# A 1-core transformer kernel: in its two memory mixers, softmax weights turned and divided by one product with a diagonal, values straight into transposed rows

## The chip, the cores and the metric

The kernel runs on one core of a Trainium2 chip. The metric is the device time of one execution in microseconds (us). Before the change the median of 3 runs is 1545.37 us (1545.18 to 1545.59).

## The reference

Four layers over 256 tokens of width 1024: an even and an odd mixer, each with a convolutional feed-forward network, then two "hybrid mixers", one with a dense and one with a mixture-of-experts network. The change touches the hybrid mixers alone. Each has three parts side by side, joined before the output projection: a gated delta rule (6 heads of 64), a forgetting attention (6 heads of 64) and a pooling part (256 columns). The forgetting attention and the join, cut to what matters:

```python
def forgetting_attention(q, k, v, f, qnorm_g, knorm_g, f_bias):
    ...
    logf = jax.nn.log_sigmoid(f.astype(F32) + f_bias.astype(F32))
    c = jnp.cumsum(logf, axis=1).transpose(0, 2, 1)
    for i in range(T // FX_BLOCK):          # FX_BLOCK = 128, T = 256
        lo, hi = i * FX_BLOCK, (i + 1) * FX_BLOCK
        s = jnp.einsum('bhqd,bhkd->bhqk', q[:, :, lo:hi], k[:, :, :hi]).astype(F32) * scale
        s = s + c[:, :, lo:hi, None] - c[:, :, None, :hi]
        s = jnp.where(k_pos <= q_pos, s, -jnp.inf)
        p = jax.nn.softmax(s, axis=-1).astype(dt)
        outs.append(jnp.einsum('bhqk,bhkd->bhqd', p, v[:, :, :hi]))
    ...
def hybrid_mixer(...):
    ...
    return jnp.concatenate([o_dn, o_fx, o_pl], axis=-1) @ w_out
```

## The kernel before

Everything is float32. The large products split both operands into a high and a low part (names ending in H and L, type fp32r) and add three products; the small products inside a mixer are plain float32. Each engine runs its own hand-written order of steps; semaphores alone tie them together. SyncE streams the weights in tiles; ScalarE copies a half tile to MWH (L2339, called by `fd(h)`: "feed up to half h"), VectorE forms the rest MWL (L3203), and TensorE multiplies (L970).

A hybrid mixer (`mixer2`, run as m0 and m1) first computes 12 input tiles (`in_half`), with the small steps of the delta rule between the halves. Then comes its tail, which this change rewrites. On TensorE, in order: `corrected_keys` (L1694), `state_in(0)`, `pooled` (L1648), `fx_turn(0)` (L1613), `state_out(1)` (L1724, L1726), `fx_scores(1)` (L1602), `pool_projected` (L1660), `state_in(1)` (L1708), `chunk_read(0, 0)` (L1737), `fx_scores(2)`, `chunk_read(0, 1)`, `fx_values(0)` (L1626), `fx_turn(1)`, `state_out(2)`, `fx_values(1)`, `state_in(2)`, `fx_turn(2)`, `state_out(3)`, `fx_values(2)`, `chunk_read(1, 0)`; then turned rows and output chunks (L1204, L970). There are three groups g of two heads. `fx_scores(g)` makes scores; VectorE adds the cumulated gates, the masks and the keys' term (L3632) and takes the maximum (L3636); ScalarE takes the exponent with its sums (L2734) into EX; `fx_turn(g)` turns the 3 blocks of 128x128 of each head with `transpose` against the identity in CS; ScalarE copies them to PT (L2742); `fx_values(g)` multiplies PT by the values FV, 64 columns at a time, into two banks with token rows. At the end VectorE divides by the sums (`attn_out`, L3283, L3290), and the result, in rows of HN, is turned by TensorE (`transposed`, L1204) and split to HTH (ScalarE, L2406) and HTL (VectorE, L3296) as chunks 3, 4, 5 of the 8 chunks of the output projection. Chunks 0, 1, 2 are the delta rule, 6 and 7 the pooling. `M2_OUT_CHUNKS` sets their order, `M2_OT` which chunks are turned together.

On VectorE the steps of this tail stand in this order: `fx_softmax(0)`, `(1)`, copies of w (L3782), `state(0)`, `new_values(1)` (L3701), `fx_softmax(2)`, `(3)`, `state(1)`, the pooling's low part (L3792), `fx_softmax(4)`, `new_values(2)`, `fx_softmax(5)`, `state(2)` (L3686, L3689), `new_values(3)`, `attn_out`, `fd(26)`, and so on. `state_out(n)` on TensorE needs `state(n - 1)`; `state_in(n)` needs `new_values(n)`. On ScalarE the scaling of the pooling's output (L2850) stands ahead of `fx_exp(1)`.

Earlier in the mixer, ScalarE copies the causal masks to MB in one instruction (L2784) and signals GpSimd, which adds the keys' term to MB by two DMAs (L898, L899). GpSimd's program runs these ahead of all its `squares_parted` steps (L851 and L853), whose results TensorE sums (L1159, L1160).

## Time and profile before

| what | us |
|---|---|
| median of 3 runs | 1545.37 |
| the profiled execution | 1544.45 |
| its span | 1542.6 |
| TensorE matmul busy | 1510.2 (98%) |
| VectorE busy | 1186.8 (77%) |
| ScalarE busy | 1015.8 (66%) |
| GpSimd busy | 69.5 (5%) |

The span runs from the first to the last instruction; 1.85 us lie around it. The granted TensorE clock is full in all 40 slices of the page. A TensorE that is busy is not one at its peak: matmuls overlap, so the distance from one start to the next is the cost of one in a stream, not its duration.

### The profile page before, as it was taken

Reading aid. Unit: us, or ns where it says so; the run is one execution under the profiler, and the core shown is the slowest. Engines: PE = TensorE matmul, PEld = TensorE weight load, DVE = VectorE, ACT = ScalarE, POOL = GpSimd, SP = SyncE. Lnnn points to the kernel's source line nnn. Section 1 sums busy time; section 2 is a strip of 40 time slices with the busy share of each in tenths; the row PEclk is TensorE's granted clock in tenths of the full one; section 3 lists DMA queues with packets and bytes.
Section 4 is the critical chain, followed back from the end, with each engine's and each line's share of the span. In section 5 each row is a group of like instructions: output and inputs, shape, how many; then the busy total and the mean of one; then the engine's idle time right before and its main releaser. Section 6 shows DMA issues by size and latency. Waiting matters only on the chain.

```text
span 1542.6 us, 27069 instructions
## 1 busy us (share of the span) xinstructions
PE 1510.2 (98%) x9988; PEld 1294.6 (84%) x9988; DVE 1186.8 (77%) x1487; ACT 1015.8 (66%) x1434; POOL 69.5 (5%) x92
## 2 busy tenths in 40 slices
PE   8999999999999999999999999999999999999998
PEld 7988888878878888899788888898778888888886
DVE  6677877775578877788675555786788888888887
ACT  5666665566566656697464445885567777777775
POOL 0000000000000000021000000220010000000000
PEclk9999999999999999999999999999999999999999
DMA  7534555545424554465255555561699999999995
GB/s 280 189 138 176 189 191 190 188 140 190 168 105 164 212 189 171 163 180 160 82 191 191 194 187 191 160 177 57 245 378 366 408 383 382 374 396 398 373 369 217
DMA packets 54795, 351.09 MB, mean 228 GB/s; under 512 B 6208, under 2 KB 9968, under 8 KB 14896
## 3 DMA queue, kind: packets, MB, share of 16 engines
q1 hardware_dynamic: 46512, 330.94, 57.3%
q0 software_dynamic: 8192, 18.90, 4.8%
q8 instruction: 62, 1.02, 0.3%
q14 instruction: 29, 0.24, 0.0%
HBM read 341.90 MB, written 7.91 MB: 227 GB/s over the span
## 4 chain that ended last, share of the span: by engine, by line
PE 90%; DVE 4%; ACT 3%; issue 1%; DMA 1%; POOL 0%; SPq 0%; DVEq 0%; ACTq 0%
PE PS L970 21%; PE PS L1944 17%; PE PS L2077 14%; PE PS L2113 11%; PE PS L1962 8%; PE PS L2078 8%; DMA W<-in_weights 1%; PE PS L1557 1%; PE PS L2048 1%; PE PS L1925 1%; ACT MWH L2339 1%; DVE MWL L3203 1%; PE PS L1153 1%; PE PS L1059 1%; PE PS L2074 0%
## 5 line engine op out<-in xcount | busy, mean ns | idle before, releaser
L3883 DVE TENSOR_TENSOR EWL<-W,EWH 128x2048 fp32r<-128x2048 f32 x144 | 329.3, 2291 | 41.9 <-ACT EWH L2894 39.7
L2077 PE MATMUL PS<-HTB,WH 128*128 128x512 f32 x944 | 329.6, 393 | 0.0
L2894 ACT ACTIVATE EWH<-W 128x2048 fp32r<-128x2048 f32 x144 | 276.8, 1923 | 56.7 <-PE PS L1962 30.3
L2078 PE MATMUL PS<-HTB,WL 128*128 128x256 f32 x1008 | 282.4, 280 | 0.0
L3195 DVE TENSOR_TENSOR WL<-W,WH 128x2048 fp32r<-128x2048 f32 x99 | 226.4, 2287 | 35.9 <-ACT WH L2315 32.8
L2315 ACT ACTIVATE WH<-W 128x2048 fp32r<-128x2048 f32 x99 | 189.3, 1918 | 98.0 <-PE PS L2078 86.6
L970 PE MATMUL PS<-MWH,HTB 128*128 128x256 f32 (+1 forms) x940 | 239.5, 340 | 2.5 <-issue 1.5
L3203 DVE TENSOR_TENSOR MWL<-W,MWH 128x1024 fp32r<-128x1024 f32 x136 | 166.7, 1239 | 68.5 <-ACT MWH L2339 66.0
L2077 PEld LDWEIGHTS PS<-HTB,WH 128*128 128x128 f32 x944 | 177.2, 188 | 40.4
L2339 ACT ACTIVATE MWH<-W 128x1024 fp32r<-128x1024 f32 x136 | 142.3, 1054 | 80.5 <-PE PS L970 72.2
L2078 PEld LDWEIGHTS PS<-HTB,WL 128*128 128x128 f32 x1008 | 189.6, 188 | 1.0
L970 PEld LDWEIGHTS PS<-MWH,HTB 128*128 128x128 f32 x940 | 162.0, 188 | 25.0 <-issue 5.6
L970 PE MATMUL PS<-MWL,HTB 128*128 128x256 f32 (+1 forms) x470 | 157.4, 335 | 0.0
L1944 PE MATMUL PS<-EWH,XH 128*128 128x512 f32 x384 | 154.7, 403 | 0.9 <-DVE EWL L3883 0.6
L1944 PE MATMUL PS<-EWL,XH 128*128 128x512 f32 x384 | 150.4, 392 | 0.0
L1944 PE MATMUL PS<-EWH,XL 128*128 128x512 f32 x384 | 149.7, 390 | 0.0
L970 PE MATMUL PS<-HTB,MWH 128*128 128x256 f32 x640 | 118.1, 286 | 1.2 <-DVE MWL L3203 1.2
L4001 DVE TENSOR_TENSOR ARENA<-ARENA,PS 128x256 f32<-128x256 f32 x124 | 46.6, 418 | 82.6 <-ACT ARENA L3005 82.6
L970 PEld LDWEIGHTS PS<-HTB,MWH 128*128 128x128 f32 x640 | 98.0, 188 | 5.3 <-issue 2.7
L970 PEld LDWEIGHTS PS<-MWL,HTB 128*128 128x128 f32 x470 | 88.5, 188 | 9.3 <-issue 0.5
L970 PE MATMUL PS<-HTB,MWL 128*128 128x256 f32 x320 | 89.3, 279 | 0.0
L1944 PEld LDWEIGHTS PS<-EWL,XH 128*128 128x128 f32 x384 | 72.0, 188 | 16.1
(432 smaller groups left out, 2430.2 us busy)
## 6 DMA issues: line engine op xcount, KB each, us to landing
W<-in_weights SPq DMA_DIRECT2D x311, 1024.0 KB, 6.5
CS<-in_consts POOLq DMA_DIRECT2D x4, 403.5 KB, 5.0
ARENA<-rows_m POOLq DMA_DIRECT2D x8, 192.0 KB, 7.0
ARENA<-rows_m POOLq DMA_DIRECT2D x2, 768.0 KB, 12.3
moe_acc<-X POOLq DMA_DIRECT2D x3, 512.0 KB, 11.9
moe_rows<-HN POOLq DMA_DIRECT2D x3, 512.0 KB, 9.9
X<-in_x SPq DMA_DIRECT2D x2, 512.0 KB, 4.2
W<-in_weights SPq DMA_DIRECT2D x2, 512.0 KB, 7.5
```

Of the source, the lines that this page charges most:

```text
L970: ins = mm(out, w if wt_first else a, a if wt_first else w, start=(start and n == 0), stop=(stop and n == 2), skip_group_check=True)
L1944: ins = mm(PS[b][:, :], x[:, e % 2, kk, :], w[sl][:, cols], start=(kk == 0 and n == 0), stop=(kk == KC - 1 and n == 2), skip_group_check=True)
L1962: ins = mm(PS[4 + hf][:, :], gh[:, gs % 2, c * P:(c + 1) * P], w[sl][:, o:o + 512], start=(gs % G_EXP == 0 and c == 0 and n == 0), stop=(g ...
L2077: mm(PS[b][:, :], WH[:, sl, o:o + P], HTB[:, :, kk, :], start=(kk == 0), stop=False, skip_group_check=True)
L2078: ins = mm(PS[b][:, 0:256], WL[:, sl, o:o + P], HTH[:, kk, :], start=False, stop=(kk == KC - 1), skip_group_check=True)
L2113: ins = mm(PS[2 * tt + hf][:, :], gh[:, gs % 2, c, tt * P:(tt + 1) * P], wt[:, sl, o:o + 512], start=(gs == 0 and c == 0 and n == 0), stop ...
L2315: A(WH[:, j % SPLIT, :], tile_ap(t), ACT.Copy).then_inc(hi_done, 2)
L2339: A(MWH[:, h % SPLIT, :], half_ap(name, h), ACT.Copy).then_inc(hi_done, 1)
L2894: A(EWH[tile % SPLIT][:, :], tile_ap(w0 + tile), ACT.Copy).then_inc(sem("moe_hi"), 1)
L3195: TT(WL[:, j % SPLIT, :], tile_ap(t), WH[:, j % SPLIT, :].bitcast(F32), SUB).then_inc(lo_done, 2)
L3203: TT(MWL[:, h % SPLIT, :], half_ap(name, h), MWH[:, h % SPLIT, :].bitcast(F32), SUB).then_inc(lo_done, 1)
L3883: TT(EWL[tile % SPLIT][:, :], tile_ap(w0 + tile), EWH[tile % SPLIT][:, :].bitcast(F32), SUB).then_inc(sem("moe_lo"), 1)
```

## The change

It does five things in both hybrid mixers. (1) The `transpose` of the softmax weights becomes a plain matmul with a diagonal of the inverse sums, which VectorE makes for each group (`fx_divided`). (2) `fx_values` has the values as the stationary operand (64 columns) and PT as the moving one, so that it leaves transposed rows, both heads of a group in the two halves of one bank; ScalarE and VectorE split them to HTH and HTL (`fx_out`, `fx_out_lo`). `attn_out` and the turning of chunks 3, 4, 5 go away. (3) Addition, masks and maximum are one `tensor_tensor_reduce` in place of two passes; the sign is turned, so the exponent has scale -1. (4) The queries' term goes into MB through a bias (`masks_of`): three heads where the copy stood, three later, and the signal to GpSimd comes after the second three. (5) The output chunks run in the order 6, 7, 3, 4, 5, 2, 0, 1, and `chunk_read(1, 1)` stands behind chunk 6. Some semaphores are shared between the two mixers.

```diff
-M2_OUT_CHUNKS = (6, 7, 4, 5, 3, 2, 0, 1)
+M2_OUT_CHUNKS = (6, 7, 3, 4, 5, 2, 0, 1)
-    M2_OT = [(4, 5), (3,), (0, 1), (2,)]
+    M2_OT = [(0, 1), (2,)]
...
             def fx_turn(g):
...
-                    pe.wait_ge(sem(m + "f_e"), h + 1)
+                    pe.wait_ge(sem("fx_divided"), 3 * l + g + 1)
                     claim(pe, key)
                     for b in range(3):
-                        ins = pe.transpose(bank(key)[:, b * P:(b + 1) * P], m2.EX[:, h % 2, b * P:(b + 1) * P], ident)
+                        over = m2.RS[:, h % 2, 0:P] if b == 0 else m2.RS[:, h % 2, P:2 * P]
+                        ins = mm(bank(key)[:, b * P:(b + 1) * P], m2.EX[:, h % 2, b * P:(b + 1) * P], over, start=True, stop=True)
...
             def fx_values(g):
...
-                        for kt in range(n + 1):
-                            b = n + kt
-                            ins = mm(bank(key)[:, h * 64:(h + 1) * 64], m2.PT[:, h % 2, b * P:(b + 1) * P], m2.FV[:, kt, h * 64:(h + 1) * 64],
-                                     start=(kt == 0), stop=(kt == n))
+                key = (m + "f", "o", g)
+                claim(pe, key)
+                for r in range(2):
+                    await_free_of(pe, (m + "f", "t", 2 * g + r))
+                for kt in range(NT):
+                    for r in range(2):
+                        h = 2 * g + r
+                        ins = mm(bank(key)[half[r], kt * P:256], m2.FV[:, kt, h * 64:(h + 1) * 64], m2.PT[:, h % 2, kt * 256:256 + kt * P],
+                                 start=(kt == 0), stop=(kt == NT - 1), skip_group_check=True)
+                done(ins, key)
...
-            for n in range(NT):
-                await_free_of(pe, (m + "f", "o", n))
+            await_free_of(pe, (m, "pz"))
+            await_free_of(pe, (m + "f", "o", 0))
+            await_free_of(pe, (m + "f", "o", 1))
+            m2_chunk(6, first=True)
+            chunk_read(1, 1)
+            m2_chunk(7)
+            m2_chunk(3)
+            m2_chunk(4)
+            for t in range(NT):
+                await_free_of(pe, (m, "o", t))
             for j in range(2):
                 transposed(m, j, M2_OT[j])
-            chunk_read(1, 1)
-            await_free_of(pe, (m, "pz"))
-            m2_chunk(6, first=True)
-            m2_chunk(7)
+            await_free_of(pe, (m + "f", "o", 2))
+            m2_chunk(5)
             for j in range(2):
                 await_free_of(pe, (m, "oT", j))
-            m2_chunk(4)
-            m2_chunk(5)
-            for t in range(NT):
-                await_free_of(pe, (m, "o", t))
-            for j in range(2, 4):
-                transposed(m, j, M2_OT[j])
-            m2_chunk(3)
-            for j in range(2, 4):
-                await_free_of(pe, (m, "oT", j))
             m2_chunk(2)
...
+            def masks_of(heads):
+                for h in heads:
+                    for n, sl in enumerate((slice(0, P), slice(P, 384))):
+                        ins = A(m2.MB[:, h, sl], cst("cmask")[:, sl], ACT.Identity, bias=st_gc[:, n, 1, h:h + 1])
+                return ins
...
-                        ins = A(m2.EX[:, h % 2, sl], m2.SM[:, h % 2, sl], ACT.Exp, bias=st_mx[:, j:j + 1], accum_out=st_sum[:, j:j + 1])
+                        ins = A(m2.EX[:, h % 2, sl], m2.SM[:, h % 2, sl], ACT.Exp, scale=-1.0, bias=st_mx[:, j:j + 1], accum_out=st_sum[:, j:j + 1])
...
+            def fx_out(g):
+                key = (m + "f", "o", g)
+                await_full(act, key)
+                out_hi(A(HTH[:, 3 + g, :], bank(key)[:, 0:256], ACT.Copy))
...
-            A(m2.MB, bc(cst("cmask"), 1, 6), ACT.Copy).then_inc(sem(m + "_gd"), 1)
+            await_free_of(act, (m, "rowT"))
+            masks_of((0, 1, 2))
...
             copied(2)
+            masks_of((3, 4, 5)).then_inc(sem(m + "_gd"), 1)
...
             fx_turned(1)
             out_square(0)
+            fx_out(0)
             fx_exp(2)
+            fx_out(1)
             fx_turned(2)
-            for j in range(2):
-                m2_out_T(m, j)
+            fx_out(2)
+            out_root(0)
             out_square(1)
-            out_root(0)
...
-                    ins = STT(m2.SM[:, h % 2, sl], bank(key)[:, sl], st_gc[:, n, 1, h:h + 1], m2.MB[:, h, sl], ADD, ADD)
-                release(ins, key)
-                await_free_of(dve, key)
-                for n, sl in enumerate((slice(0, P), slice(P, 384))):
-                    ins = dve.tensor_reduce(st_mx[:, 2 * h + n:2 * h + n + 1], m2.SM[:, h % 2, sl], AX.X, MAX, negate=True)
+                    ins = dve.tensor_tensor_reduce(m2.SM[:, h % 2, sl], bank(key)[:, sl], m2.MB[:, h, sl], -1.0, -NEG, ADD, MIN,
+                                                   st_mx[:, 2 * h + n:2 * h + n + 1])
                 ins.then_inc(sem(m + "f_mx"), 1)
+                dve.wait_ge(sem(m + "f_mx"), h + 1)
+                dve.sem_inc(free[uses[key][0]], 1)
+
+            def fx_divided(g):
+                dve.wait_ge(sem(m + "f_e"), 2 * g + 2)
+                link(dve.reciprocal(st_ri[:, 4 * g:4 * g + 4], st_sum[:, 4 * g:4 * g + 4]))
+                over = m2.RS[:, :, 0:256].rearrange("p u (n q) -> p u n q", n=2)
+                share = st_ri[:, 4 * g:4 * g + 4].rearrange("p (u n) -> p u n", u=2)
+                TT(over, bc(bc(ident, 1, 2), 1, 2), bc(share, 3, P), MUL).then_inc(sem("fx_divided"), 1)
...
             fx_softmax(0)
             fx_softmax(1)
+            fx_divided(0)
...
+            fx_divided(1)
             fx_softmax(4)
             new_values(2)
             fx_softmax(5)
+            fx_out_lo(0)
             state(2)
+            fx_divided(2)
             new_values(3)
-            attn_out(m + "f", 6, 64, 384)
+            fx_out_lo(1)
+            out_sums(0)
             fd(26)
-            for j in range(2):
-                out_lo((m, "oT", j), M2_OT[j][0], len(M2_OT[j]))
-            out_sums(0)
+            fx_out_lo(2)
```

## Rows read from the trace of the kernel before

**Rows 1.** The page: busy time, share of the span and instructions of each engine.

```profile
PE 1510.2 (98%) x9988; PEld 1294.6 (84%) x9988; DVE 1186.8 (77%) x1487; ACT 1015.8 (66%) x1434; POOL 69.5 (5%) x92
```

**Rows 2.** Windows over the two tails: length, busy us (x instructions), clock, DMA.

```profile
733.90:759.40 25.50, 23.03 (x434) 19.41 (x433) 16.97 (x46) 14.34 (x42) 0.00 (x0) 1.00 0.08 31
...
1056.00:1081.40 25.40, 22.93 (x433) 19.35 (x432) 16.90 (x46) 14.28 (x42) 0.00 (x0) 1.00 0.08 33
```

**Rows 3.** Groups of TensorE by form, whole span: busy us, mean ns | idle before.

```profile
L1626 PE MATMUL PS<-ARENA 128*128 128x64 f32 x72 | 9.3, 279 | 0.0
...
L1613 PE MATMUL PS<-CS,ARENA 128*128 128x128 f32 x36 | 5.6, 282 | 1.2 <-ACT ARENA L2734 1.2
```

**Rows 4.** Timeline of TensorE, tail of m0: start us, length us, [idle before <-releaser].

```profile
741.16 1.18 PE L1648 MATMUL PS<-CS,ARENA 128*64 128x130 f32 x16
742.27 0.87 PE L1613 MATMUL PS<-CS,ARENA 128*128 128x128 f32 x6
...
744.35 0.93 PE L1602 MATMUL PS<-ARENA 64*128 64x128 f32 x8 [0.70 <-ACT ARENA L2742]
...
745.48 0.60 PE L1660 MATMUL PS<-ARENA,PR 64*64 64x256 f32 x4
...
748.89 1.55 PE L1626 MATMUL PS<-ARENA 128*128 128x64 f32 x12
750.28 0.82 PE L1613 MATMUL PS<-CS,ARENA 128*128 128x128 f32 x6
...
755.75 1.55 PE L1626 MATMUL PS<-ARENA 128*128 128x64 f32 x12
758.09 0.84 PE L1204 MATMUL PS<-CS,HN 128*128 128x128 f32 x6 [0.29 <-issue]
759.36 0.50 PE L970 MATMUL PS<-MWH,HTB 128*128 128x512 f32 x1
```

**Rows 5.** Timeline of ScalarE, same tail.

```profile
742.22 0.19 ACT L2734 ACTIVATION_READ_ACCUMULATOR ARENA<-ARENA,STAT 128x1 f32 x1
...
746.34 0.84 ACT L2850 ACTIVATE HTB<-PS,PR 128x256 fp32r<-128x256 f32 x2 [1.75 <-PE PS L1660]
...
753.73 0.40 ACT L2734 ACTIVATE ARENA<-ARENA,STAT 128x128 f32<-128x128 f32 x1 [0.80 <-DVE STAT L3636]
...
754.53 0.18 ACT L2734 ACTIVATION_READ_ACCUMULATOR ARENA<-ARENA,STAT 128x1 f32 x1
```

**Rows 6.** Timeline of VectorE, same tail.

```profile
737.07 0.74 DVE L3632 SCALAR_TENSOR_TENSOR ARENA<-PS,STAT,ARENA 128x128 f32<-128x128 f32 x2 [1.15 <-PE PS L1602]
...
738.38 0.73 DVE L3632 SCALAR_TENSOR_TENSOR ARENA<-PS,STAT,ARENA 128x128 f32<-128x128 f32 x2
...
752.32 0.73 DVE L3632 SCALAR_TENSOR_TENSOR ARENA<-PS,STAT,ARENA 128x128 f32<-128x128 f32 x2
...
756.70 0.23 DVE L3283 RECIPROCAL STAT<-STAT 128x12 f32<-128x12 f32 x1
756.97 1.02 DVE L3290 TENSOR_TENSOR HN<-PS,STAT 128x384 f32<-128x384 f32 x2
```

**Rows 7.** Groups of VectorE by form: a product of the diagonal's size.

```profile
L4012 DVE TENSOR_TENSOR ARENA<-ARENA 128x512 f32<-128x512 f32 x11 | 7.6, 693 | 1.1
```

**Rows 8.** Timeline of ScalarE, input tiles of m0.

```profile
686.80 2.13 ACT L2784 ACTIVATE ARENA<-CS 128x2304 f32<-128x2304 f32 x1
...
703.49 1.06 ACT L2339 ACTIVATE MWH<-W 128x1024 fp32r<-128x1024 f32 x1 [2.38 <-PE PS L970]
```

**Rows 9.** Timeline of GpSimd, input tiles of m0.

```profile
690.14 2.06 POOL L899 DMA_DIRECT2D ARENA<-rows_m  x1
695.09 0.61 POOL L851 CAST M2SQH<-ARENA 128x512 fp32r<-128x512 f32 x1 [2.88 <-ACT ARENA L2345]
695.78 1.28 POOL L853 TENSOR_TENSOR M2SQL<-ARENA,M2SQH 128x512 fp32r<-128x512 f32 x1
```

**Rows 10.** Timeline of TensorE: the sums that use these squares.

```profile
708.52 0.39 PE L1160 MATMUL PS<-M2SQL,BLR 128*128 128x512 f32 x1
```

More of the change, by code:

```diff
@@ L428, in plan_m2 @@
         pair("w")
-        for n in range(NT):
-            plan((m + "f", "o", n), 2 + n)
+        for g in range(2):
+            plan((m + "f", "o", g), 2 + g)
         for t in range(NT):
@@ L446, in plan_m2 @@
         rot((m, "vp", 3))
+        rot((m + "f", "o", 2))
         rot = Rot([6, 7])
-        for j in range(4):
+        for j in range(2):
             rot((m, "oT", j))
@@ L1609, in fx_turn @@
                     key = (m + "f", "t", h)
-                    pe.wait_ge(sem(m + "f_e"), h + 1)
+                    pe.wait_ge(sem("fx_divided"), 3 * l + g + 1)
                     claim(pe, key)
                     for b in range(3):
-                        ins = pe.transpose(bank(key)[:, b * P:(b + 1) * P], m2.EX[:, h % 2, b * P:(b + 1) * P], ident)
+                        over = m2.RS[:, h % 2, 0:P] if b == 0 else m2.RS[:, h % 2, P:2 * P]
+                        ins = mm(bank(key)[:, b * P:(b + 1) * P], m2.EX[:, h % 2, b * P:(b + 1) * P], over, start=True, stop=True)
                     done(ins, key)
             def fx_values(g):
-                for h in (2 * g, 2 * g + 1):
-                    await_free_of(pe, (m + "f", "t", h))
-                    for n in range(NT):
-                        key = (m + "f", "o", n)
-                        if h == 0:
-                            claim(pe, key)
-                        for kt in range(n + 1):
-                            b = n + kt
-                            ins = mm(bank(key)[:, h * 64:(h + 1) * 64], m2.PT[:, h % 2, b * P:(b + 1) * P], m2.FV[:, kt, h * 64:(h + 1) * 64],
-                                     start=(kt == 0), stop=(kt == n))
-                        if h == FX_H - 1:
-                            done(ins, key)
+                key = (m + "f", "o", g)
[8 more added lines that the diff above has]
+                done(ins, key)
             def sums_of(i):
@@ L1803, in mixer2 @@
             chunk_read(1, 0)
-            for n in range(NT):
-                await_free_of(pe, (m + "f", "o", n))
+            await_free_of(pe, (m, "pz"))
[8 more added lines that the diff above has]
+                await_free_of(pe, (m, "o", t))
             for j in range(2):
                 transposed(m, j, M2_OT[j])
-            chunk_read(1, 1)
-            await_free_of(pe, (m, "pz"))
-            m2_chunk(6, first=True)
-            m2_chunk(7)
+            await_free_of(pe, (m + "f", "o", 2))
+            m2_chunk(5)
             for j in range(2):
-                await_free_of(pe, (m, "oT", j))
-            m2_chunk(4)
-            m2_chunk(5)
-            for t in range(NT):
-                await_free_of(pe, (m, "o", t))
-            for j in range(2, 4):
-                transposed(m, j, M2_OT[j])
-            m2_chunk(3)
-            for j in range(2, 4):
                 await_free_of(pe, (m, "oT", j))
@@ L2687, in row_columns @@
                 rows = bank(rowT)[:, 0:48].rearrange("p (t j h) -> p t j h", t=2, j=4)
-                A(st_gc[:, :, 0, :], rows[:, :, 0, :], ACT.Copy).then_inc(sem(m + "_gc"), 1)
+                A(st_gc[:, :, 0, :], rows[:, :, 0, :], ACT.Copy).then_inc(sem("m2_gc"), 1)
                 A(st_gc[:, :, 1, :], rows[:, :, 3, :], ACT.Copy)
@@ L2863, in mixer2 @@
             fd(28)
-            for j in range(2, 4):
+            for j in range(2):
                 m2_out_T(m, j)
@@ L3562, in decayed @@
             def decayed():
-                dve.wait_ge(sem(m + "_dec"), 1)
+                dve.wait_ge(sem("m2_dec"), l + 1)
                 for r in range(2):
@@ L3661, in row_less @@
             def row_less():
-                dve.wait_ge(sem(m + "_gc"), 1)
+                dve.wait_ge(sem("m2_gc"), l + 1)
                 dve.wait_ge(sem(m + "_gd"), 1)
@@ L3809, in mixer2 @@
             fd(28)
-            for j in range(2, 4):
+            for j in range(2):
                 out_lo((m, "oT", j), M2_OT[j][0], len(M2_OT[j]))
```

8 lines of the change are left out of this document (6 added, 2 removed).

## The prediction

> **What bounds the kernel.** I read the page's busy shares first: TensorE's matmuls cover 98% of the span, VectorE 77%, ScalarE 66% [rows 1]. So time moves only where TensorE gets other work or another wait. Then the windows over the two tails that the change rewrites: 25.5 and 25.4 us, TensorE busy 23.0 and 22.9, clock at its upper level (1.00, that is 2.4 GHz), DMA share 0.08 [rows 2]. The tails are alike, so what one is worth counts twice, and DMA is out of it. TensorE's timeline shows that even there it waits for others: for an eviction ahead of the second scores (0.70 us), and, between the last values and the turning of the attention's rows, from 755.75 plus the values' work to 758.09 [rows 4]. ScalarE waits 0.80 for the maximum of the last head [rows 5]. That makes the tail a chain through three engines, three rounds long (one for each group g), and not a plain stream of matmuls. I therefore laid out both programs step by step in their written order from these rows, with starts spaced as in the rows and 0.06 to 0.15 us for each hand-over, which is what the rows leave between an end and the start it releases.
>
> **Price of each part.**
>
> *Product for transpose.* The groups by form show 36 records for the 36 transposes of both mixers (2 mixers, 6 heads, 3 blocks), but 72 for the 36 plain float32 products of the values: a plain product is two instructions [rows 3]. Six transposes start in 0.80 us, and twelve instructions of the values in 1.39 (748.89 to 750.28) [rows 4]: 0.11 to 0.12 each for either. So 18 more instructions, +2.0 us of TensorE for each mixer; a group takes 1.45 in place of 0.80. The Trainium skill ("TensorE: Matmul & The Clock Gate", section Terms) calls the transpose mode 4 times faster for FP32; the rows show 2 times at this width, and by the page's factor the sum below would be 8 us worse.
>
> *Values into transposed rows.* For a group, two heads with 256 and 128 moving columns, two instructions each. The heads write different halves of the 128 output rows. The pooling's products do the same, and 16 of them with some 130 columns start in 1.11 us, 0.07 each: two run at once [rows 4]. Four instructions of 256 columns in two pairs take 0.60 with the last one's length, 0.22 a pair [rows 4]. So 2 x 0.22 + 2 x 0.11 and a start of 0.1: 0.75 a group against 1.39 to 1.55, -0.7 each. Without the overlap 1.4, no gain.
>
> *Turning of chunks 3 to 5.* Six transposes go (-0.8), with the wait for `attn_out` ahead of them: its division started at 756.97 and held TensorE to 758.09 [rows 4, 6]. In place of it stand `fx_out` on ScalarE (0.4 each) and `fx_out_lo` on VectorE (0.4 each).
>
> *Maximum in one pass.* Two passes cost 1.31 us a head (737.07 to 738.38) [rows 6]. One pass is at least the first of them, 0.74, and at most 1.3, if a reducing instruction runs at half the pace. I take 0.93, the addition's row and 0.09 for each of two accumulator reads, as ScalarE's follow its exponents [rows 5]. The Trainium skill says so too ("VectorE: DVE Perf Modes", section on two Vector instructions with no wait between them): an accumulator output is a second instruction; no row of VectorE here shows one.
>
> *The diagonal, a new wait.* `fx_divided(g)` needs the sums of both heads; then reciprocal 0.23 (0.27 to the next start) and a product of 128x512, 0.69 [rows 6, 7]: 0.96 us, and 1.1 until TensorE starts. Before, the first head was turned while the second was in its exponent. Behind this wait on VectorE are queued the copies of w and `state(0)`, then `fx_softmax(4)`, then `new_values(3)`.
>
> *MB in two parts.* The first six activations take about what the one copy took (2.13) [rows 8]. The second six, 2.1, fit the 2.38 us for which ScalarE waits before 703.49 [rows 8]: no cost there. But GpSimd's signal comes at 703.2, not 688.9. Its two DMAs occupy it for 0.9 + 2.06, to 706.6, and only then the parting of the squares starts: 0.69 to the second step, 1.28 for it [rows 9], done at 708.6. TensorE wants it at 708.52 [rows 10]: 0.1 us late with the hand-over, 1 us if the DMAs' issue is slow, 0 at best. The DMAs land long before the masks are needed at 737.07 [rows 6].
>
> **The three rounds** (m0; m1 is the same).
> Round 0: the exponents of heads 0 and 1 end at 742.41 [rows 5]; diagonal 743.4; turning starts at 743.5 instead of 742.27 and takes 0.65 more. The state's step follows at 744.95. The 0.70 wait ahead of the second scores is now covered, as the first head is evicted by then, so they start at 745.4 against 744.35: +1.05.
> Round 1: the scaling of the pooling's output, which stands ahead of the exponents on ScalarE, starts at 747.4 instead of 746.34 [rows 5]. It takes 0.73, two heads' exponents 1.85 (0.88 to 0.99 each, by 753.73 to 754.53 and its read), so 749.98. Diagonal at 751.0, turning at 751.1 against 750.28: +0.85, after its longer run +1.5. The cheaper values(0) and values(1) lie beside waits and bring nothing.
> Round 2: `new_values(2)` waits for the late state, so `fx_softmax(5)` starts at 753.97 instead of 752.32 [rows 6]. Its maximum is there at 754.9, the exponents end at 755.9 (before: 754.71 [rows 5]), VectorE is through with `state(2)` at 756.1, diagonal 757.05, turning 757.15 to 758.6. This is the largest stall: TensorE has nothing from 754.6 on. The last values start at 759.4 against 755.75: +3.65.
> Then it gets back. Values 0.8 shorter; no wait and no turning of three chunks. Before, 3.61 us went from the last values to chunk 6 at 759.36 [rows 4]; now 0.75 + 0.37, so 760.5: +1.15. `chunk_read(1, 1)` (0.5) now stands behind chunk 6: +1.65. From there the work is equal: four chunks, six transposes, two chunks. I see no new wait: the gated rows are ready at 769.5 and needed at 771.9.
> My layout of the old program comes 0.15 late at these marks, so +1.5, with GpSimd's +0.1: **+1.6 us a mixer, +3.2 in all**.
>
> **Forecast.** 1544.45 + 3.2 = 1547.65 for the profiled execution; the median of the runs was 0.92 above it, so 1548.6 us.
>
> **Rivals.**
> *A, the waits don't form (faster).* If VectorE's shorter passes draw the chain ahead so that the diagonals are ready when TensorE comes, only work counts: +2.0 of turning, -2.0 of values, -0.8 of turning chunks, -0.5 of wait: -1.3 a mixer, 1545.37 - 2.6 = 1542.8. It decides in round 2, from the point at which both last exponents end by 753.6, so that the diagonal is there at 754.7. Against it: they ended at 754.71 before [rows 5] with an earlier start, and the diagonal's 1.1 comes on top.
> *B, the one-pass maximum is no faster.* At 1.3 us a head the softmax of heads 3 and 5 is later; by the same layout +1.2 more a mixer: 1551.0.
> *C, the values' halves don't overlap.* Only values(2) is on the path: +0.65 a mixer, 1549.9; with values(1), 1551. This is also the case in which the change does not do what it says. Against it the pooling's products.
> *D, the skill's factor 4.* A product would cost four transposes, 0.45 in place of 0.22, 18 on the path: +4.0 a mixer, 1556.6. The records of the values speak against it.
> *E, GpSimd is late by 1 us a mixer:* 1550.4.
>
> **How the numbers follow.** A measurement of this kernel can tell about 0.2%, 3.1 us, from no change. Forecast 0.62, A 0.15, B 0.08, C 0.07, D 0.02, E 0.06. The forecast's own spread is about +-2 us (0.3 for each of three diagonals, 0.4 for the hand-overs, on two mixers), centred on +3.2, so it gives slower 0.33, same 0.27, faster 0.02. A gives faster 0.10, same 0.05. The rest gives slower 0.17, same 0.06. Together faster 0.12, same 0.38, slower 0.50. The range 1543.5 to 1551.5 leaves out D, half of A, and the upper edge of B, C and E. The forecast's own range is 1546.6 to 1550.6.
>
> **What the new profile would show.** In each tail: 36 records of the turning product and 24 of the values; L1613's successor idle for VectorE's diagonal, about 1.2, 0.8 and 2.5 us; no turning of rows ahead of chunk 6; chunk 6 at about 760.5. A mean of the one-pass maximum over 0.65 us for 256 columns would show B; starts of the values 0.11 apart or more would show C; an idle time of TensorE at the sums of squares would show E. I am wrong if the second and third rounds wait under 0.5 us, or if a wait appears between chunks 4 and 5 for the gated rows.

## The result, and the profile after

The changed kernel takes 1551.9 us (1551.3 to 1555.2) against 1545.3 of the kernel before on the same chip: a ratio of 1.0045, interval 1.0035 to 1.0055, 6.6 us. In a second series it took 1553.6 (1551.0 to 1556.2), ratio 1.0055 (1.0042 to 1.0067). The forecast was 1548.6 with a range to 1551.5: the sign was right, the size not. Two executions took over 2100 us at a mean granted clock of 0.56 and 0.65 (one of the kernel before beside `e1_masks_early`, one of `g1_sums_by_ones`) and are left out of every ratio.

The profiled execution took 1551.84 us with a span of 1549.9, 7.3 more than the span before. The page's busy line, against [rows 1]: TensorE is busy only 2.6 us more. The rest is waiting, in the tails and at the sums of squares.

```profile
PE 1512.8 (98%) x9988; PEld 1295.5 (84%) x9988; DVE 1181.8 (76%) x1495; ACT 1020.7 (66%) x1458; POOL 70.9 (5%) x92
```

Windows over the two tails, from "qk" (L1541, the 48 small products of queries and keys that close the input tiles) to chunk 6, as in [rows 2]. Length, busy of PE, PEld, DVE, ACT, POOL, clock, DMA:

```profile
734.60:760.98 26.38, 22.04 (x421) 18.17 (x420) 13.90 (x50) 14.86 (x43) 0.00 (x0) 1.00 0.08 32
1059.60:1085.90 26.30, 21.95 (x421) 18.15 (x420) 13.87 (x50) 14.83 (x43) 0.00 (x0) 1.00 0.08 31
```

They are 0.9 us longer, with TensorE busy a microsecond less: 4.3 idle where 2.5 was. The groups by form answer to [rows 3, 7] and price each new operation (busy, mean ns | idle before):

```profile
L1615 PE MATMUL PS<-ARENA 128*128 128x128 f32 x72 | 9.6, 284 | 6.3 <-DVE ARENA L3657 6.3
L1627 PE MATMUL PS<-ARENA 128*64 128x256 f32 x24 | 3.9, 400 | 0.7 <-ACT ARENA L2746 0.7
L1627 PE MATMUL PS<-ARENA 128*64 128x128 f32 x24 | 2.4, 273 | 0.0
...
L3645 DVE CUSTOM_DVE_ANT_0 ARENA<-PS,ARENA 128x256 f32<-128x256 f32 x12 | 5.0, 418 | 0.0
L3657 DVE TENSOR_TENSOR ARENA<-CS,STAT 128x512 f32<-128x512 f32 x6 | 4.2, 692 | 0.2
L3645 DVE CUSTOM_DVE_ANT_0 ARENA<-PS,ARENA 128x128 f32<-128x128 f32 x12 | 3.5, 288 | 3.6 <-PE PS L1603 2.5 <-DVE STAT L3645 0.9
```

The turning product is 72 records for 36 blocks, as forecast, and it waits 6.3 us in six places for the diagonal. TensorE's timeline of m0's tail shows the three rounds, against [rows 4]:

```profile
744.12 1.60 PE L1615 MATMUL PS<-ARENA 128*128 128x128 f32 x12 [1.06 <-DVE ARENA L3657]
...
746.18 0.93 PE L1603 MATMUL PS<-ARENA 64*128 64x128 f32 x8
...
750.35 0.87 PE L1627 MATMUL PS<-ARENA 128*64 128x256 f32 x8
751.74 1.60 PE L1615 MATMUL PS<-ARENA 128*128 128x128 f32 x12 [0.52 <-DVE ARENA L3657]
...
757.41 1.60 PE L1615 MATMUL PS<-ARENA 128*128 128x128 f32 x12 [1.54 <-DVE ARENA L3657]
...
759.69 0.87 PE L1627 MATMUL PS<-ARENA 128*64 128x256 f32 x8 [0.16 <-ACT ARENA L2746]
760.49 0.56 PE L1737 MATMUL PS<-ARENA 64*64 64x64 f32 x12
760.98 0.50 PE L971 MATMUL PS<-MWH,HTB 128*128 128x512 f32 x1
```

Two losses lie outside the tails. In the input tiles GpSimd is late, against [rows 9, 10]; the first four rows are its timeline, the last two TensorE's, in m0 and in m1:

```profile
703.23 1.51 POOL L899 DMA_DIRECT2D ARENA<-rows_m  x1 [27.19 <-ACT ARENA L2727]
704.14 2.06 POOL L900 DMA_DIRECT2D ARENA<-rows_m  x1
705.00 2.45 POOL L852 CAST M2SQH<-ARENA 128x512 fp32r<-128x512 f32 x1
707.54 1.26 POOL L854 TENSOR_TENSOR M2SQL<-ARENA,M2SQH 128x512 fp32r<-128x512 f32 x1
...
708.95 0.47 PE L1160 MATMUL PS<-M2SQH,BLR 128*128 128x512 f32 x1 [1.13 <-POOL M2SQL L854]
...
1033.92 0.47 PE L1160 MATMUL PS<-M2SQH,BLR 128*128 128x512 f32 x1 [1.13 <-POOL M2SQL L854]
```

And behind the tails the granted clock falls from 1.00 (2.4 GHz) to its lower level, 0.50 (1.2 GHz), for some 4 us at a time: once at the router and once in the first expert. The page doesn't show this: a slice is 39 us long and its digit 9 stands for 90% or more, here as before the change. In windows of 4 us, the clock is the third number from the end:

```profile
1112.00:1116.00 4.00, 2.81 (x24) 2.02 (x25) 2.82 (x8) 1.62 (x9) 0.93 (x2) 0.87 0.98 372
1116.00:1120.00 4.00, 3.85 (x17) 3.03 (x16) 2.67 (x10) 3.97 (x3) 0.00 (x0) 0.71 0.97 396
1136.00:1140.00 4.00, 2.53 (x17) 2.23 (x17) 2.46 (x7) 2.31 (x3) 1.07 (x1) 0.85 0.69 256
1140.00:1144.00 4.00, 4.00 (x14) 3.12 (x14) 3.61 (x3) 2.77 (x4) 0.00 (x0) 0.72 0.85 309
```

The same eight products of 256 columns, in the changed kernel:

```profile
1114.70 3.54 PE L1020 MATMUL PS<-X,CS 128*128 128x256 f32 x8
```

and in the profiled execution of the kernel before, whose only fall comes in the last 4 us of its span, behind TensorE's last product:

```profile
1109.44 1.97 PE L1019 MATMUL PS<-X,CS 128*128 128x256 f32 x8
```

**Where the time went.** I set the start of each group of TensorE against that of the same group before, and read the lateness at four marks: the first input tile of a memory mixer (685.0 and 1007.3 before), qk (733.9, 1056.0), the turning of the output's rows (770.4, 1092.4) and the experts. It goes -0.27, +0.72, +2.38; +2.42, +3.63, +5.22; +5.26 at the router, +6.39 at the first expert, +6.97 behind it, +7.3 at the end. So: input stages 0.99 and 1.21, tails 1.66 and 1.59, clock 1.13 and 0.6. The experiments below give such differences.

**The clock of every execution.** Each execution was also timed with its mean granted clock. In the profiles at hand a mean of 0.999 went with no fall or one ahead of the end, 0.998 with one, 0.997 with one or two, less with longer or more falls. Sorted by it, the executions of the kernel before (83, beside four series of experiments) and of the changed kernel (12, both series) are:

| mean clock | before: number, median us | changed: number, median us |
|---|---|---|
| 0.999 | 24, 1544.9 | none |
| 0.998 | 20, 1545.5 | 1, 1551.0 |
| 0.997 | 23, 1546.5 | 4, 1551.9 |
| 0.996 or less | 16, 1548.7 | 7, 1553.6 |

The kernel before falls too: 39 of its 83 executions stand at 0.997 or less, against 11 of 12 of the changed kernel. At equal clock the change costs 4.9 to 5.5 us, close to the tails' 3.25 and the input stages' 2.2 together; the rest of the 6.6 us is that the clock is down more often.

### The profile page after: what moved, and what is told of

It reads as the page before. It is cut to its first block, busy times and chain, and to the rows that moved or that the text cites. A ratio compares the mean times of both kernels' runs of the same rounds, so it can differ in the third digit from the quotient of the medians.

```text
span 1549.9 us, 27115 instructions
## 1 busy us (share of the span) xinstructions
PE 1512.8 (98%) x9988; PEld 1295.5 (84%) x9988; DVE 1181.8 (76%) x1495; ACT 1020.7 (66%) x1458; POOL 70.9 (5%) x92
## 4 chain that ended last, share of the span: by engine, by line
PE 90%; DVE 3%; ACT 3%; issue 1%; POOL 1%; DMA 0%; DVEq 0%; ACTq 0%; SPq 0%; POOLq 0%
PE PS L971 20%; PE PS L1941 17%; PE PS L2074 14%; PE PS L2110 11%; PE PS L1959 8%; PE PS L2075 8%; PE PS L2045 1%; PE PS L1922 1%; ACT MWH L2336 1%; PE PS L1615 1%; PE PS L1558 1%; DVE MWL L3216 1%; PE PS L1154 1%; PE PS L1060 1%; PE PS L1033 0%
```

## The experiments

"Tail" is the added time from qk to the turning of the rows, against the kernel before, in m0 and m1.

### Four parts undone, one at a time

`e1_masks_early`: the masks of all heads where heads 0 to 2 are.

```diff
-            masks_of((0, 1, 2))
+            masks_of(range(6)).then_inc(sem(m + "_gd"), 1)
...
-            masks_of((3, 4, 5)).then_inc(sem(m + "_gd"), 1)
```

> The changed kernel with the masks of all six heads written where those of heads 0 to 2 are (the place of the old single copy), and the signal to GpSimd given there. Theory (late GpSimd: sums of squares 0.76 us later at 708.95, input stage 1.0 us longer in mixer 0 and 1.2 in mixer 1): both transfers into MB are issued about 7 us earlier, the sums start at about 708.2 again and qk at about 733.9, so 2.2 us less than the changed kernel: about 1549.7. Rival 1 (GpSimd's lateness is not on the path): no change, 1551.9. Rival 2 (ScalarE's 2.2 us of masks are on the path at the earlier place): sums as early, but input tiles later, 1551 to 1553.

1550.6 us (1547.9 to 1555.0), ratio 1.0031 (1.0013 to 1.0049). The sums no longer wait, and m1's input stage is 0.04 us longer than before instead of 1.21; m0's is 0.64, since the masks are now one block of 4.27 us on ScalarE, ahead of the next tile. The gain of 1.3 us is little over half of the 2.2 expected, and the median lies between the theory's 1549.7 and the range of rival 2. Part of the rest is a clock fall in m0's tail (window 756 to 760), which grew by 2.96 us where it grew by 1.66 in the changed kernel:

```profile
756.00:760.00 4.00, 2.46 (x17) 2.32 (x13) 1.56 (x5) 1.33 (x5) 0.00 (x0) 0.66 0.00 0
```

`e2_no_product_no_diagonal`:

```diff
-                    pe.wait_ge(sem("fx_divided"), 3 * l + g + 1)
+                    pe.wait_ge(sem(m + "f_e"), h + 1)
...
-                        ins = mm(... m2.EX[...], over, start=True, stop=True)
+                        ins = pe.transpose(... m2.EX[...], ident)
...
-            fx_divided(0)
```

> The changed kernel with the weights turned by three transposes a head as before, each head as soon as its exponentials are there, and no reciprocal and diagonal on VectorE. It leaves out the division of the softmax. Theory (the product and the wait for the diagonal are what lengthens the tails): turning groups at 0.8 instead of 1.6 us, VectorE 0.96 us a round free, and the wait gone: 3 us less a mixer, about 1546, chunk 6 about 3 us nearer to qk in both mixers (23.3 instead of 26.3 us). Rival (the tail is set by the softmax passes and the evictions): under 1 us a mixer, 1550 or more.

1541.4 us, ratio 0.9971 (0.9961 to 0.9981): 10.5 less than the changed kernel, more than the 6 expected. Tails -2.96 and -2.91. What is left of the change (one pass, values into transposed rows, no turning of three chunks) stands 2.9 us a mixer below the kernel before, but this kernel divides nowhere, so a part of the 2.9 is the division it leaves out. Product and diagonal cost 4.6.

`e3_two_passes`:

```diff
-                    ins = dve.tensor_tensor_reduce(m2.SM[...], bank(key)[:, sl], m2.MB[:, h, sl], -1.0, -NEG, ADD, MIN, st_mx[...])
+                    ins = TT(m2.SM[...], bank(key)[:, sl], m2.MB[:, h, sl], ADD)
+                release(ins, key)
...
+                    ins = dve.tensor_reduce(st_mx[...], m2.SM[:, h % 2, sl], AX.X, MAX, negate=True)
```

> The changed kernel with the one-pass sum and maximum parted into an addition and a reduction again (masks still hold the gate's column). Theory (the one pass saves 0.4 us a head on VectorE, and most of VectorE's softmax lies on the chain of the tail): 1.5 to 2.5 us more a mixer, about 1556. Rival (softmax is covered by TensorE): under 0.5 us a mixer, 1552 to 1553.

1555.3 us, ratio 1.0064 (1.0047 to 1.0081): 3.4 more than the changed kernel, within the 3 to 5 expected. Both tails had a fall (they grew by 3.95 and 3.74), so not all of it is VectorE. One pass starts a head every 0.83 us, two passes every 1.19, in VectorE's timeline:

```profile
738.29 0.62 DVE L3645 TENSOR_TENSOR ARENA<-PS,ARENA 128x128 f32<-128x128 f32 x2 [1.15 <-PE PS L1603]
...
739.48 0.61 DVE L3645 TENSOR_TENSOR ARENA<-PS,ARENA 128x128 f32<-128x128 f32 x2
```

`e4_transposes_behind_diagonal`: the transposes of e2 with the wait and the diagonals kept.

```diff
-                        ins = mm(... m2.EX[...], over, start=True, stop=True)
+                        ins = pe.transpose(... m2.EX[...], ident)
```

> The changed kernel with transposes against the plain identity in place of the product, still behind the wait for the diagonal, which VectorE still makes. It leaves out the division. It measures the product alone. Theory (two instructions for one, about 0.8 us a group, on the path in at least two of three rounds): 1.5 to 2.4 us less a mixer, about 1548. Rival (the diagonal's wait is the whole loss): under 0.5 us a mixer, 1551 or more.

1551.1 us (1547.8 to 1555.0), ratio 1.0029 (1.0016 to 1.0042). Read alone it says that the product is free. Its profile, taken of its slowest execution, says otherwise: the clock fell twice in m0's tail and once, for longer, in m1's (and once at 16 to 24 us, far ahead of both), and the tails grew by 3.1 and 3.0 us:

```profile
748.00:752.00 4.00, 4.00 (x50) 2.58 (x41) 2.35 (x11) 0.43 (x2) 0.00 (x0) 0.57 0.01 4
760.00:764.00 4.00, 3.70 (x51) 2.81 (x52) 2.45 (x6) 1.66 (x5) 0.00 (x0) 0.74 0.00 0
...
1086.00:1090.00 4.00, 3.82 (x47) 2.71 (x43) 3.48 (x6) 1.25 (x5) 0.00 (x0) 0.53 0.00 0
```

### The waits filled, and product and diagonal taken apart

`e5_waits_filled` (the changed kernel) and `e7_transposes_waits_filled` (the kernel of e4, with 8, 5, 12):

```diff
+                key = (m + "f", "t", 2 * g)
+                claim(pe, key)
+                for k in range((8, 4, 12)[g]):
+                    pe.transpose(bank(key)[:, 0:P], ident, ident)
                 for h in (2 * g, 2 * g + 1):
```

> The changed kernel with TensorE kept at work while it waits for the diagonals: 8, 4 and 12 extra transposes of the identity (0.11 us each, into the bank that the turned weights then overwrite) ahead of the three turning groups of each mixer, whose waits were 1.06, 0.52 and 1.54 us. Nothing else changes. Theory (the granted clock falls because the change empties TensorE in the tails; a fall costs 1.1 to 1.9 us, and falls in some runs and not in others make the spread of 1547.9 to 1555 us): no fall in either tail, spread of the runs under 3 us, median 1550 to 1551. Rival 1 (falls have another cause): same spread, 1552. Rival 2 (the extra transposes delay the product): up to 1 us a mixer more, 1553.

1551.5 us (1550.8 to 1553.9), ratio 1.0041 (1.0027 to 1.0055). Tails 1.64 and 1.60, without a fall, as the unfilled profile had them: filling costs the tails nothing. The median is 0.4 us lower, which can't be told from nothing, and the spread is 3.1 us where under 3 was expected. One fall stayed, at 1138 to 1142. Two of the 5 executions stand at a mean clock of 0.997 or less, where 11 of 12 of the unfilled kernel do.

> The kernel of transposes behind the diagonal (it leaves out the division), with the waits filled by 8, 5 and 12 extra transposes as in the run before. That kernel ran at 1551.1 us (1547.8 to 1555.0) and its profile had the clock at half around 748, 760 and 1088 us. Theory (it would have gained 1.5 to 2.4 us a mixer over the changed kernel, and clock falls gave it back): falls gone, about 1548. Rival (the product is not on the path; the gain was never there): 1551.

1548.7 us (1547.7 to 1549.6), ratio 1.0014 (1.0004 to 1.0023). The median is 2.4 us below e4's and the spread 2 us instead of 7, though the intervals of the two ratios overlap. The gain is one of the clock and of nothing else: at a mean clock of 0.998 e4 took 1547.8 and this kernel 1547.7 and 1548.0, at 0.997 e4 1549.0 and this kernel 1548.1 to 1549.6. But 4 of e4's 6 executions stand at 0.995 or less, none of these 10. This profile has no fall in either tail; one is left at 1135 to 1139. Tails +0.06 and +0.04: against e5's 1.6 the product alone is worth 1.6 us a mixer, which e4 had hidden.

`e8_product_with_identity` and `e9_diagonal_not_waited_for`: the product against the plain identity, waiting for `f_e` alone; e9 keeps the calls of `fx_divided` on VectorE.

```diff
-                    pe.wait_ge(sem("fx_divided"), 3 * l + g + 1)
+                    pe.wait_ge(sem(m + "f_e"), h + 1)
...
-                        ins = mm(... m2.EX[...], over, start=True, stop=True)
+                        ins = mm(... m2.EX[...], ident, start=True, stop=True)
```

> The changed kernel with the turning done by the product, but with the plain identity on its right and no diagonal made or waited for (it leaves out the division). Against the run with transposes and no diagonal (1541.4) it measures the product alone. Theory (0.8 us a group, three groups, on the path in most): 1.6 to 2.4 us a mixer more, 1545 to 1546, so that product and diagonal share the loss of 10.5 us at about 4 and 6. Rival (the product is covered): under 0.5 us a mixer, 1542.

> The changed kernel with the product taken with the plain identity as soon as a head's exponentials are there, while VectorE still waits for both heads' sums and makes the diagonal, which nobody reads (the division is left out). Without diagonal: 1544.7; with diagonal and wait: 1551.9. Theory (VectorE's own time and its wait for the exponentials, ahead of softmax(4), new_values(2) and new_values(3), are the larger part of the 7.2 us): 1548.5 to 1550. Rival (TensorE's wait is the larger part): 1545 to 1547.

e8 1544.7 us, ratio 0.9995 (0.9986 to 1.0005); e9 1546.9, ratio 1.0005 (0.9995 to 1.0014). With e2 and the changed kernel this is a ladder:

| step | median us | tails, us |
|---|---|---|
| e2: transposes, no diagonal | 1541.4 | -2.96, -2.91 |
| e8: product instead | 1544.7 | -1.69, -1.70 |
| e9: VectorE makes the diagonal, unread | 1546.9 | -0.59, -0.58 |
| changed kernel: TensorE waits for it | 1551.9 | +1.66, +1.59 |

None of the four profiles has a fall in a tail, so the tails can be compared; the medians are of different chips and hold the falls elsewhere. So a mixer pays 1.2 to 1.3 us for the product, 1.1 for VectorE's time and 2.2 for the wait. e9 is the rival's case: the wait is the larger part, not VectorE's time.

### The clock: timing, gaps or emptier tails

`d1_before_shifted` (the kernel before) and `f1_router_filled` (the changed one):

```diff
+            if m == "m1":
+                claim(pe, (m, "oT", 0))
+                for k in range(48):
+                    pe.transpose(bank((m, "oT", 0))[:, 0:P], ident, ident)
```

> The kernel before with 48 transposes of the identity (0.11 us each, 5.2 us of busy TensorE) in the tail of mixer 1, ahead of the transposes of its output rows; the router and the experts behind it are untouched, and reached as late as in the changed kernel. Theory (the same idle gaps of 0.88, 0.58 and 1.47 us let the clock fall or not by the instant at which they come): the granted clock falls at the router or at the first experts (1112 to 1142 us) where the kernel before had 1.00, and the time is 5.2 plus 1 to 2 us over that of before: 1551.5 to 1552.5. Rival (the changed kernel's falls come from its emptier tails): no fall there, 1550.5.

1550.6 us (1549.7 to 1552.0), ratio 1.0026 (1.0016 to 1.0037). The rival's number: the profiled execution is 5.2 us late at every mark behind the insertion, and no more. The router's gaps are the same (0.87 and 0.59 us) at the same instants as in the changed kernel, and the clock stays up. The instant alone does not make the fall; 7 of the 8 executions stand at a mean clock of 0.998 or more.

```profile
1112.55 1.07 PE L998 MATMUL PS<-HT,STAT 128*32 128x256 f32 x16 [0.87 <-DVE HT L3128]
1114.21 0.58 PE L1007 MATMUL PS<-STAT,ARENA 128*128 128x8 f32 x4 [0.59 <-ACT ARENA L2221]
1114.64 1.97 PE L1019 MATMUL PS<-X,CS 128*128 128x256 f32 x8
```

> The changed kernel with 7 and 4 extra transposes of the identity in the router's two gaps (0.88 and 0.58 us, ahead of the logit parts and of the logits). Theory (the fall at 1114 to 1118, 1.1 us, hangs on these gaps): no fall there, 1 to 1.5 us less than the changed kernel, about 1550.7; the fall at 1138 may stay. Rival (it falls all the same, at this place or at the next): 1551.9.

1553.7 us, ratio 1.0047 (1.0030 to 1.0064). The filling itself costs the router 0.5 us. No fall there or behind it, but one in each tail, whose code is that of the changed kernel; they grew by 3.07 and 2.86 us. All four executions stand at 0.997. The clock fell all the same, at another place.

`h3_before_with_unread_diagonal`: the kernel before, with `fx_divided(g)` called on VectorE where the change calls it.

```diff
+            def fx_divided(g):
...
+                dve.wait_ge(sem(m + "f_e"), 2 * g + 2)
+                ri = m2.RS[:, 0, 256 + 4 * g:260 + 4 * g]
+                link(dve.reciprocal(ri, st_sum[:, 4 * g:4 * g + 4]))
+                TT(over, bc(bc(ident, 1, 2), 1, 2), bc(share, 3, P), MUL)
```

> The kernel before with the reciprocals and the diagonals of the changed kernel made on VectorE at the same places, written to memory that nobody reads; TensorE never waits for them itself. Theory (VectorE is held up, by 0.96 us a round and by waits for the exponentials, and TensorE empties): 1.5 to 3 us a mixer more, 1548.5 to 1551.5, and at least one fall of the clock before the end, in a tail or behind it. Rival (falls are unrelated to the tails): no fall, 1545.4 plus what VectorE costs.

1548.4 us (1547.1 to 1556.0), ratio 1.0018 (1.0007 to 1.0030). Nothing was added to TensorE and nothing waits for the diagonal. The profiled execution has a fall in each tail, which grew by 1.95 and 2.07 us:

```profile
746.00:750.00 4.00, 4.00 (x42) 3.02 (x40) 3.76 (x12) 1.50 (x5) 0.00 (x0) 0.58 0.02 4
...
1070.00:1074.00 4.00, 4.00 (x47) 3.02 (x40) 3.59 (x11) 1.11 (x4) 0.00 (x0) 0.61 0.01 4
```

That looks like the theory, but the executions don't bear it out. Five of 11 stand at 0.997 or less, and so do 11 of 23 of the kernel before in the same series; 3 stand at 0.999. Those three took 1547.4 to 1547.9, some 3 us over the kernel before at the same clock (1544.7), so VectorE's delay costs time of itself, about 1.5 us a mixer, and that it brings falls is not shown.

`after_again`: the changed kernel once more.

> The changed kernel once more, for the places of its clock falls. Theory (falls hang on small differences in timing between executions): 1551.9 again, but in this profile the falls are at other places than 1114 and 1138, or of another number. Rival (they are fixed by the program): falls at 1114 to 1118 and 1138 to 1142 again.

1553.6 us, where 1551.9 was expected. Its falls are at 1084 to 1088, inside m1's tail, which grew by 2.83 instead of 1.59, and at 1138 to 1145; none at the router. The falls move between executions of one program.

```profile
1084.00:1088.00 4.00, 4.00 (x50) 2.84 (x49) 2.45 (x5) 1.55 (x5) 0.00 (x0) 0.57 0.02 4
...
1112.00:1116.00 4.00, 2.54 (x31) 1.76 (x28) 3.11 (x5) 2.58 (x8) 1.61 (x3) 1.00 0.74 272
```

`h1_transfers_behind_squares`:

```diff
+        def masks_in(m):
+
+            rows = ROWS[m]
             pool.wait_ge(sem(m + "_gd"), 3)
             pool.dma_start(m2.MB[:, :, 0:P], rows[2, :, 0:P].partition_broadcast(P), accum_op=ADD).then_inc(sem(m + "_mb_in"), 16)
...
                 squares_parted(st[1])
+                masks_in(st[1])
```

> The changed kernel with GpSimd's two transfers into MB issued after its last sums of squares instead of ahead of them; they are needed 25 us later. Theory (GpSimd's lateness is 1.0 and 1.2 us of the input stages, all of it on TensorE's path): sums at about 708.2 with no idle ahead of them, about 2.2 us less than the changed kernel, 1549.7. Rival (the lateness is taken up elsewhere): under 0.7 us less, 1551.2 or more.

1550.0 us (1548.0 to 1554.1), ratio 1.0035 (1.0023 to 1.0047). The profiled execution was its fastest, 1548.0, and has no fall before the end. There the sums are on time again:

```profile
707.73 0.50 PE L1165 MATMUL PS<-M2SQH,BLR 128*128 128x512 f32 x1
```

It stands at -0.28 at m0's first input tile, -0.46 at m0's qk and +1.58 behind the tail (which is 0.4 longer than in the changed kernel; the transfers are now issued from 725.9 on and land so late that the first softmax waits for them, to 739.45), at +1.64, +1.68 and +3.28 in m1, and at +3.28 at TensorE's last product. So the input stages cost nothing any more, and the tails cost 2.04 and 1.60. This is the forecast's own case; its profiled time is 1548.0 against 1547.65, with some luck, since this execution began 0.3 early and its first tail was the longer one. The median is 1550.0, 1.4 above the forecast's 1548.6.

### Versions meant to beat both

`g1_sums_by_ones`: the division moved behind the values.

```diff
+                        ins = mm(bank(key)[half[r], 256 + kt * P:512], ones[:, 0:64], m2.PT[...], ...)
...
+                link(dve.reciprocal(m2.RS[:, 0, 0:256], bank(key)[:, 256:512]))
+                link(TT(m2.RS[:, 1, 0:256], bank(key)[:, 0:256], m2.RS[:, 0, 0:256], MUL))
```

> A version meant to beat both: the one pass, the masks early, transposes for the turning, values straight into transposed rows, and the division where they leave the bank: four more products a pair of heads with a block of ones give every row the sum of its column's weights, VectorE takes the reciprocal (128x256) and multiplies. Theory (the diagonal is bad because turning waits for it; behind the values it has 5 us of slack ahead of chunk 3): close to the run without any division (1541.4) plus TensorE's 0.75 us a group: 1542 to 1544. Rival (VectorE's 0.84 us a group fall on the state updates or the last read): 1546.

1552.5 us, ratio 1.0039 (1.0024 to 1.0054), worse than the rival too. m0's tail had a fall besides. The price I had given the reciprocal was a product's. It takes four times that, and chunk 6 waits for VectorE to leave the bank. VectorE's groups, then TensorE's row:

```profile
L3657 DVE RECIPROCAL ARENA<-PS 128x256 f32<-128x256 f32 x6 | 10.5, 1755 | 0.1
...
L3658 DVE TENSOR_TENSOR ARENA<-PS,ARENA 128x256 f32<-128x256 f32 x6 | 2.5, 425 | 0.2
```

```profile
760.77 0.77 PE L971 MATMUL PS<-MWH,HTB 128*128 128x512 f32 x1 [2.29 <-DVEq L3659]
```

`e6_before_with_one_pass` and `h2_before_one_pass_masks_parted`: the kernel before with the one pass; the masks in one block or in two.

```diff
-                    ins = STT(m2.SM[...], bank(key)[:, sl], st_gc[...], m2.MB[:, h, sl], ADD, ADD)
...
+                    ins = dve.tensor_tensor_reduce(m2.SM[...], bank(key)[:, sl], m2.MB[:, h, sl], -1.0, -NEG, ADD, MIN, st_mx[...])
...
-            A(m2.MB, bc(cst("cmask"), 1, 6), ACT.Copy).then_inc(sem(m + "_gd"), 1)
+            masks_of(range(6)).then_inc(sem(m + "_gd"), 1)
```

> The kernel before with the one-pass sum and maximum alone (masks hold the gate's column, all six heads written by ScalarE where the single copy was). Theory (the one pass is a gain of about 1.5 to 1.8 us a mixer, as the run with two passes showed from the other side; the early masks cost ScalarE and so the input tiles about 0.4 us a mixer): about 1542.5. Rival (in the kernel before, TensorE and not VectorE holds up the scores): 1545 to 1546.

> The version meant to beat both: the kernel before (transposes, values in rows, division where they leave the bank) with the one pass alone, the masks written in two parts where the changed kernel has them, and the two transfers behind GpSimd's squares. With all masks early it ran at 1543.7 and its input stages were up to 0.8 us late. Theory: masks in ScalarE's gaps give that back, 1542 to 1543. Rival (the masks cost ScalarE the same at either place): 1543.7.

e6 1543.7 us (1543.0 to 1545.6), ratio 0.9985 (0.9975 to 0.9994), tails -1.15 and -1.14; h2 1544.2, ratio 0.9988 (0.9979 to 0.9997). Both beat the kernel before, by about 2 us, and the changed one by 8. In h2, whose transfers stand behind the squares as in h1, m0's scores are held up by 1.0 us, so the masks' place made no difference that can be told from this run, which was expected at 1542 to 1543.

## Where the prediction was right, and why it was wrong

**The tails: right.** Forecast +1.5 us a mixer, measured 1.66 and 1.59 (2.04 and 1.60 in h1). The marks hold to half a microsecond. With m0's lateness at qk (0.72) taken off, the turnings start at 743.40, 751.02 and 756.69 (forecast 743.5, 751.1, 757.15), the second scores at 745.46 (745.4), the last values at 758.97 (759.4), chunk 6 at 760.26 (760.5). Some of the closeness is luck: from chunk 6 to the turning of the rows the changed kernel takes 0.76 us longer, not 0.5. The third wait, forecast at about 2.5, is 1.54, with another 0.42 ahead of `state_in(2)`, which I had starting without a wait; the second is 0.52, just over the 0.5 below which I would have been wrong. The product is two instructions and takes 1.56 us a group from its start to the next one's (forecast 1.45). The one pass starts a head every 0.83 us (0.93). The values' halves overlap: eight instructions in 0.87. (Round 1's "+0.85" is 0.82 by its own times, 751.1 against 750.28; the sum doesn't use it.) So A, B, C and D are out. The Trainium skill's factor of 4 for the transpose mode ("TensorE: Matmul & The Clock Gate", section Terms) does not hold at this width: six blocks take 1.60 us as products and 0.87 as transposes [rows 4], a factor of 2. The Trainium skill's accumulator output as a second instruction ("VectorE: DVE Perf Modes", section on two Vector instructions with no wait between them) agrees with VectorE's timeline, 0.08 us for each read:

```profile
738.06 0.42 DVE L3645 CUSTOM_DVE_ANT_0 ARENA<-PS,ARENA 128x256 f32<-128x256 f32 x1
738.40 0.08 DVE L3645 DVE_READ_ACCUMULATOR2_ANT STAT<- 128x1 f32 x1
```

**First failing step: "to 706.6, and only then the parting of the squares starts ... 0.1 us late with the hand-over".** This term was sized at 0.1 us a mixer. It is 1.0 us in m0 and 1.2 in m1, 2.2 us in all against 0.2, and by itself lifts the forecast from 1548.6 to 1550.6. Three things add up. TensorE waits for the parted squares ahead of both products, so the need was the first one's 708.19 and not the low one's 708.52, and this execution reached it 0.27 earlier. The CAST did not wait for the end of the transfers but started at 705.00, beside the second, and took 2.45 us instead of 0.61; it ended at 707.45, where I had 707.3. The low part ended at 708.80, not 708.6, and the sums started 0.15 behind it. I had given "1 us if the DMAs' issue is slow" as the bound and E a chance of 0.06; for the input stages E is what happened. h1, which moves the two transfers alone, took it away.

**Second failing step: the forecast had no term for the clock.** I read "clock at its upper level" over the tails and took it over to the new program. The 0.92 us between the profiled execution and the median went in without a cause; by the executions' clocks it goes with the falls that the kernel before has in about half of its executions, and the changed kernel has more. With the first step put right and a clock that stays up, 1550.6 would have been left, inside the range; the falls are what is left up to 1551.9. In the profiled execution of the changed kernel two falls cost 1.1 and 0.6 us; in a tail one costs 1.2 to 1.4 (e1, f1, after_again against the undisturbed 1.6), and after_again's in the first expert cost 1.8 (from +6.95 to +8.74). Why one fall costs more than another was not looked into. With the tails' 3.25, GpSimd's 2.2, the clock's 1.7, -0.27 at the start and 0.3 at the end all but 0.1 of the 7.3 us is accounted for.

**What the runs settle about the falls, and what not.** Neither the instant (d1) nor the router's gaps (f1) decide. The falls are not fixed by the program, since after_again and h1 have the same code as the changed kernel in the tails and behind them, and falls at other places, or none. The changed kernel has more of them than the kernel before (11 of 12 executions at 0.997 or less against 39 of 83), and with the waits filled they are rarer again (8 of 15 in e5 and e7, against 16 of 18 in the changed kernel and e4). That speaks for the empty stretches in the tails as a cause, but does not show it: moving the transfers alone also went with fewer (2 of 6 in h1), and shorter tails do not keep them away. e2 and e8 stand 2.9 and 1.7 us a tail below the kernel before, and their profiles have falls behind the tails, in e2 here:

```profile
1128.00:1132.00 4.00, 2.89 (x7) 2.34 (x8) 2.18 (x3) 4.00 (x5) 1.07 (x1) 0.60 0.91 302
```

Why the clock falls at one place and not at another stays open.

**The parts of the change.** The one pass is a gain of some 1.1 us a tail by itself (e6), less what the masks cost ScalarE. e2's tails, with transposed values and fewer turnings, stand 1.8 us below e6's; how much of this is the layout and how much the division that e2 leaves out, no run parts. The division by a product with a diagonal costs 4.6 a mixer, of which 3.3 are work and a wait of VectorE and TensorE that the old division, at the end of the chain, did not have.

## What to carry to other kernels

A scaling folded into a product is free only if the factor is there early. Here the factor is the last thing that the softmax yields, so a step that could start a head at a time now waits for both heads and an operation on another engine, three times in a row. When a signal is moved, look at what its waiter does next, not only at what it sends: two small transfers held the squares back. And when a change thins out TensorE, compare profiles of equal clock before reading a gain or a loss of a few microseconds; e4's median alone would have called the product free. A profile shows one execution; where the mean clock of every execution is at hand, sort by it first.

## What the runs showed of the hardware

- The same program runs at different mean clocks from execution to execution: 0.995 to 0.999 for the kernel before, with medians from 1544.9 us at 0.999 to 1548.7 at 0.996 and less. A fall inside the program lasts 4 to 7 us and cost 0.6 to 1.8 us. Extra transposes in TensorE's waits went with fewer deep falls (e7: none of 10 executions at 0.995 or less, e4: 4 of 6) and a median 2.4 us lower.
- VectorE's reciprocal takes 1.76 us for 128x256, its product 0.42. From 12 columns (0.23 [rows 6], in other memory) to 256 that is 6.3 ns a column; the one pass goes from 0.29 to 0.42 for 128 more, 1.0 ns a column. The Trainium skill ("VectorE: DVE Perf Modes", the walkthrough of the 8-slice pipeline) has it iterate with a repeat count of 8, which points the same way.
- A sum with its minimum in one pass costs hardly more than the sum: 0.42 and 0.08 for 256 columns, against 0.41 for the addition alone in e3 and another 0.41 for its maximum.
- GpSimd's CAST of 128x512 took 2.45 us beside the issue of a transfer, in both mixers, and 0.61 alone [rows 9]. No run parts the issue from what the other engines did at the time.
